# A two-layer transformer on one core: the last expert quad by column halves, the layer border rewritten tile by tile, and the loads of layer 1 in another order

## The reference

```python
c_act = silu(c)
for l in range(2):
    mod = c_act @ mod_w[l] + mod_b[l]                     # 6 rows of 1024
    shift1, scale1, gate1, shift2, scale2, gate2 = split(mod, 6)
    h = rms_norm(x, norm1_g[l]) * (1 + scale1) + shift1
    mix = diff_fox_mixer(h, ...) if l == 0 else stick_breaking_mixer(h, ...)
    x = x + gate1 * mix
    h = rms_norm(x, norm2_g[l]) * (1 + scale2) + shift2
    x = x + gate2 * hier_moe(h, ...)                      # 4 groups of 8 experts

def stick_breaking_mixer(h, w_in, w_out):                 # 16 heads of 64
    q, k, v = split(h @ w_in, 3)
    z = q k^T / 8;  log_keep = where(mask, log_sigmoid(-z), 0)
    later = reverse cumsum(log_keep) - log_keep
    a = where(mask, exp(log_sigmoid(z) + later), 0)
    return (a @ v) @ w_out

hid = silu(h @ w1[e]) * (h @ w3[e])                       # per expert, D=1024 -> 512
y  += (hid * gate) @ w2[e]                                # 512 -> 1024
```

## Time and profile before

| | us |
|---|---|
| median of three runs | 1255.74 (1253.07 to 1257.35) |
| the profiled execution, its own time | 1254.81 |
| its span on the core | 1252.7 |
| PE busy | 909.3 |
| DVE busy | 299.1 |
| ACT busy | 197.6 |
| DMA, mean over the span | 391 GB/s |

### The profile page before, as it was taken

How to read it: one execution, slowest core, us unless ns; L and a number is a source line. 1 busy time by engine, 2 the same in 40 slices (tenths; PEclk the granted TensorE clock), 3 DMA queues, 4 the chain that set the end, 5 groups by cost and what they waited for, 6 DMA issues and landing times.

```text
span 1252.7 us, 13436 instructions
## 1 busy us (share of the span) xinstructions
PE 909.3 (73%) x5515; PEld 419.7 (34%) x5515; DVE 299.1 (24%) x596; ACT 197.6 (16%) x410; POOL 14.9 (1%) x81
## 2 busy tenths in 40 slices
PE   7999999656565556484889999957556565655578
PEld 3445555122221212131348664522121222213133
DVE  1578634001010101010137555501010010101011
ACT  2213414010100100000020454311010101000000
POOL 4000000000000000000000000000000000000000
PEclk9999999788788878777999999988787888877879
DMA  9998897999999999999999936889999999999997
GB/s 357 362 397 280 326 387 279 419 427 427 431 428 427 427 429 429 429 426 428 419 400 408 370 129 268 345 353 428 428 426 428 429 429 429 427 428 426 428 424 303
DMA packets 74605, 489.95 MB, mean 391 GB/s; under 512 B 18092, under 2 KB 18228, under 8 KB 47680
## 3 DMA queue, kind: packets, MB, share of 16 engines
q1 hardware_dynamic: 74256, 488.25, 94.8%
q10 hardware_dynamic: 304, 1.07, 0.3%
HBM read 488.25 MB, written 1.05 MB: 391 GB/s over the span
## 4 chain that ended last, share of the span: by engine, by line
DMA 49%; PE 43%; DVE 3%; SPq 2%; issue 1%; ACT 1%; DVEq 0%; ACTq 0%
DMA tokens<-in_moe_w_dram 46%; PE bank L1128 13%; PE bank L810 8%; PE bank L1161 5%; PE bank L1009 5%; PE bank L863 4%; SPq L510 2%; DMA ring<-in_moe_w_dram 2%; PE bank L738 1%; DMA ring<-in_mod_w_dram 1%; PE bank L931 1%; PE bank L947 1%; PE bank L1095 1%; PE bank L796 1%; PE bank L1172 1%
## 5 line engine op out<-in xcount | busy, mean ns | idle before, releaser
L1128 PE MATMUL bank<-ring,region 128*32 128x512 f32 x1456 | 263.1, 675 | 173.1 <-DMA tokens<-in_moe_w_dram 91.8
L1161 PE MATMUL bank<-ring,region 128*32 128x512 f32 x832 | 143.9, 719 | 131.9 <-DMA ring<-in_moe_w_dram 77.7
L1128 PEld LDWEIGHTS bank<-ring,region 128*32 128x32 f32 x1456 | 69.3, 122 | 351.9 <-issue 288.5
L1128 PE MATMUL bank<-work,region 128*32 128x512 f32 x256 | 134.1, 685 | 0.0
L1128 PE MATMUL bank<-tokens,region 128*32 128x512 f32 x256 | 134.0, 685 | 0.0
L2123 DVE TENSOR_TENSOR region<-region,bank 128x512 f32<-128x512 f32 x16 | 11.0, 688 | 443.6 <-PE bank L1128 443.6
L810 PE MATMUL bank<-ring,tokens 128*128 128x512 f32 x256 | 114.3, 596 | 0.6 <-ACT tokens L1378 0.6
L1161 PEld LDWEIGHTS bank<-ring,region 128*32 128x32 f32 x832 | 37.2, 129 | 224.2 <-issue 189.3
L2133 DVE TENSOR_TENSOR region<-bank,region 128x512 f32<-128x512 f32 x32 | 22.1, 692 | 262.8 <-PE bank L1161 262.8
L1378 ACT ACTIVATE region<-bank,shift,scale 128x128 f32<-128x128 f32 x64 | 24.1, 457 | 358.4 <-PE bank L1115 358.4
L1115 PE MATMUL bank<-region,h 128*128 128x128 f32 x512 | 64.1, 287 | 9.1 <-issue 8.3
(11 more groups left out here) (280 smaller groups left out, 930.0 us busy)
## 6 DMA issues: line engine op xcount, KB each, us to landing
ring<-in_moe_w_dram SPq DMA_DIRECT2D x132, 2048.0 KB, 19.5
work<-in_moe_w_dram SPq DMA_DIRECT2D x22, 2048.0 KB, 24.3
tokens<-in_moe_w_dram SPq DMA_DIRECT2D x22, 2048.0 KB, 28.6
ring<-in_mod_w_dram SPq DMA_DIRECT2D x20, 2048.0 KB, 13.8
ring<-in_moe_w_dram SPq DMA_DIRECT2D x8, 1536.0 KB, 13.5
ring<-in_od_w_in_dram SPq DMA_DIRECT2D x5, 2048.0 KB, 15.0
ring<-in_mod_w_dram SPq DMA_DIRECT2D x8, 1024.0 KB, 14.4
ring<-in_ev_w_in_dram SPq DMA_DIRECT2D x4, 2048.0 KB, 17.7
```

Of the source, the lines that this page charges most:

```text
L1128: last = pe.matmul(bank[which][32 * j:32 * j + 32, :], m.seated[:, k, 32 * j:32 * j + 32], weights(4 * which + j, k * FE), start=(k == 0), ...
L1161: last = pe.matmul(bank[half][32 * j:32 * j + 32, :], m.hidT[:, c, 32 * j:32 * j + 32], w, start=(c == 0), stop=(c == FC - 1), skip_group_ ...
```

## The change

Three things, in the words of the code:

- **Last quad of a layer.** The last three w2 units come as column halves: first half of c = 1, 2, 3, then the second halves, the very last one in two quarters of 256 columns. TensorE multiplies the first columns for all c and gives these results back at once, then does the other half in two quarters of 256 columns (banks 1 and 2). VectorE makes y in three pieces, the last two of 256 columns.
- **Layer border.** VectorE copies the first halves of x after its last piece of y; ScalarE takes the squares by halves, one of them straight from PSUM; VectorE scales both tiles; the modulation is done in pieces of 128x128, tile by tile, and the first projection takes the pieces in the order in which they come.
- **Order of the loads of layer 1.** `DENSE_ORDER[1]` is another, and three steps at which TensorE and VectorE deal with the `SECOND` sums are put three later.

```diff
-               [("in", 0), (GATE1, 0), (GATE1, 1), ("in", 1), (SECOND, 0), ("in", 2), (SECOND, 1), (SECOND, 2),
-                (SECOND, 3), ("in", 3), ("in", 4), ("in", 5)] + GATE_THEN_OUT]
+               [("in", 0), ("in", 1), ("in", 2), (GATE1, 0), (GATE1, 1), (SECOND, 0), (SECOND, 1), ("in", 3),
+                (SECOND, 2), (SECOND, 3), ("in", 4), ("in", 5)] + GATE_THEN_OUT]
-SECOND_PART_AT = (12, 2)
-SECOND_COLS_AT = (13, 4)
+SECOND_PART_AT = (12, 5)
+SECOND_COLS_AT = (13, 7)
-ADD_SUMS_AT = (17, 1)
+ADD_SUMS_AT = (17, 4)
...
+            landed(8)
+            products_of(0, 0, 0, COL)
+            products_of(0, 1, COL, T)
+            products_of(0, 2, COL + T, T).then_inc(used, 1)
+            for c in range(1, FC):
+                if c >= 2:
+                    keep_clock(3, 3)
+                pe.wait_ge(m.half_full[c - 1], 16 * (l + 1))
+                last = products_of(c, 0, 0, COL)
+            last.then_inc(e["y_half"], 1)
+            pe.wait_ge(e["y_copied"], copied)
+            give_back(0, COL, (end_sem, 1))
+            for c in range(1, FC - 1):
+                if c == 2:
+                    keep_clock(3, 3)
+                landed(8 + c)
+                products_of(c, 1, COL, T)
+                products_of(c, 2, COL + T, T).then_inc(used, 1)
+            keep_clock(3, 3)
+            pe.wait_ge(m.last_full, 16 * (l + 1))
+            products_of(FC - 1, 1, COL, T).then_inc(e["y_half"], 1)
+            landed(QUAD_UNITS - 1)
+            products_of(FC - 1, 2, COL + T, T).then_inc(used, 1)
+            pe.wait_ge(e["y_copied"], copied + 1)
+            give_back(COL, T)
+            pe.wait_ge(e["y_copied"], copied + 2)
+            give_back(COL + T, T, (end_sem, TT))
...
-            if halves and c >= 2:
-                keep_clock(3, 5 if c == 2 else 3)
...
-            keep_clock(2, 10)
+            keep_clock(2, 4)
             turn_tokens(2 * l)
-            keep_clock(2, 2)
+            keep_clock(2, 1)
...
+    def norm_sums():
+        for t in range(TT):
+            act.wait_ge(s["dve_took"], t + 1)
+            chain.link(fn(m.h[:, t, 0:COL], m.x[:, t, 0:COL], ACT.Square, accum_out=m.sq_sum[:, 2 + t:3 + t]))
+            chain.link(fn(m.sq_sum[:, 4 + t:5 + t], m.sq_sum[:, 2 + t:3 + t], ACT.Identity, scale=1.0 / D,
+                          bias=m.eps[:, 0:1]))
+        for t in range(TT):
+            if t == 0:
+                act.wait_ge(m.moe[0, "end"], 2)
+                fn(m.h[:, 0, COL:D], bank[6][:, :], ACT.Square, accum_out=m.sq_sum[:, 0:1]).then_inc(s["act_took"], 1)
+                act.wait_ge(s["act_took"], 1)
+            else:
+                act.wait_ge(s["dve_took"], 3)
+                chain.link(fn(m.h[:, 1, COL:D], m.x[:, 1, COL:D], ACT.Square, accum_out=m.sq_sum[:, 1:2]))
...
+    def take_sums(l):
+        for t in range(1 if l + 1 == DEPTH else TT):
+            dve.wait_ge(m.moe[l, "end"], 1)
+            dve.tensor_copy(m.x[:, t, 0:COL], bank[4 + t][:, :]).then_inc(s["dve_took"], 1)
...
+        dve.wait_ge(m.moe[l, "end"], 3)
+        dve.tensor_copy(m.x[:, 1, COL:D], bank[7][:, :]).then_inc(s["dve_took"], 1)
+        dve.wait_ge(s["act_took"], 1)
+        dve.tensor_copy(m.x[:, 0, COL:D], bank[6][:, :]).then_inc(s["x_added"], TT)
...
+        for t in range(TT):
+            dve.wait_ge(s["rstd_done"], 3 + t)
+            ts(m.h[:, t, :], m.x[:, t, :], m.rstd[:, t:t + 1], None, ALU.mult).then_inc(
```

More of the change, by code:

```diff
@@ L1144, in quad_of_experts, with products_of, give_back @@
         pe.wait_ge(e["turned_copied"], 2 * n + 2)
+        def products_of(c, b, lo, n):
+            for j in range(4):
+                last = pe.matmul(bank[b][32 * j:32 * j + 32, 0:n], m.hidT[:, c, 32 * j:32 * j + 32],
+                                 weights(8 + c, j * D + lo, n), start=(c == 0), stop=(c == FC - 1),
+                                 skip_group_check=True, tile_position=(0, 32 * j))
+            return last
+        def give_back(lo, n, end=None):
+            half, col = divmod(lo, COL)
+            for t in range(TT):
+                last = pe.matmul(bank[4 + 2 * half + t][:, col:col + n], m.back[:, t, :], m.y_seat[:, lo:lo + n],
+                                 start=False, stop=end is not None, skip_group_check=True)
+                if end is not None and t >= TT - end[1]:
+                    last.then_inc(end[0], 1)
@@ L1146, in quad_of_experts @@
+        if lead_fill:
+            pe.wait_ge(m.lead_full, lead_fill)
+        for j in range(4):
+            landed(8 + j)
         for c in range(FC):
-            if c == 0 and not halves:
-                if lead_fill:
-                    pe.wait_ge(m.lead_full, lead_fill)
+            for half in range(2):
                 for j in range(4):
-                    landed(8 + j)
-            if halves and c >= 2:
-                keep_clock(3, 5 if c == 2 else 3)
[L1154 to L1161, removed]
+                    last = pe.matmul(bank[half][32 * j:32 * j + 32, :], m.hidT[:, c, 32 * j:32 * j + 32],
+                                     weights(8 + j, c * D + half * COL),
@@ L1169, in quad_of_experts @@
         for half in range(2):
[L1170 to L1175, removed]
+            pe.wait_ge(e["y_copied"], 2 * n + half + 1 + ended)
+            give_back(half * COL, COL)
     def experts(l):
@@ L1642, in program_scalar @@
     for half in range(OUT_UNITS):
-        act.wait_ge(m.moe[DEPTH - 1, "end"], half + 1)
-        act.copy(m.x[:, 1, half * COL:(half + 1) * COL], bank[5 + 2 * half][:, :]).then_inc(s["y1_ready"], 1)
+        act.wait_ge(m.moe[DEPTH - 1, "end"], 2 * half + 1)
+        act.copy(m.x[:, 1, half * COL:(half + 1) * COL], bank[5 + 2 * half][:, :]).then_inc(s["act_took"], 1)
 def backwards(ap):
@@ L2126, in quad_of_experts @@
             e["turned_copied"], 1)
-        for half in range(OUT_UNITS):
-            if half == 0:
-                dve.wait_ge(e["y_half"], n + 1)
+        ended = l if path == "first" else 0
+        pieces = ((0, 0, COL), (1, COL, T), (2, COL + T, T)) if last else ((0, 0, COL), (1, COL, COL))
+        for i, (b, lo, cols) in enumerate(pieces):
+            if i + 1 < len(pieces):
+                dve.wait_ge(e["y_half"], n + 1 + ended + i)
             else:
                 wait_used(dve, m, l, path, n, 12)
-            cols = slice(half * COL, (half + 1) * COL)
-            tt(m.y_seat[:, cols], bank[half][:, :], m.gate2[:, cols], ALU.mult).then_inc(e["y_copied"], 1)
+            tt(m.y_seat[:, lo:lo + cols], bank[b][:, 0:cols], m.gate2[:, lo:lo + cols], ALU.mult).then_inc(
+                e["y_copied"], 1)
+        if last:
+            return
         dve.wait_ge(e["gate_made"], n + 1)
```

129 lines of the change are left out of this document (77 added, 52 removed).

## The result

The changed kernel takes 1275.72 us (median of 4 runs, 1273.24 to 1276.35) against 1255.7 before (1253.07 to 1257.35): a ratio of 1.0163, with a 95% interval of 1.0147 to 1.0180. It is slower by 20 us. The forecast was 1271.5, with a range from 1264 to 1277. Its profiled execution took 1276.27, with a span of 1274.5 against 1252.7.

The account below looks back on a forecast made before the run. Bound: PE in layer 1's dense stage, bytes in its expert stage. Terms -1.6 + 13.5 + 1.0 - 0.55 + 1.7 + 2.3 = +16.35 on 1254.81 gave 1271.2, stated as 1271.5; range 1264 to 1277.

Parts of the forecast that it names:

- the order of loads: Layer 1 dense stage: late third SECOND unit delays VectorE's sums and heads; TensorE waits 14.4 us, second scores +13.5.
- The clock's term: Work behind TensorE's wait in layer 1's dense stage runs partly at 1.2 GHz: +1.7 us, ends 0.5 and 4.
- 1.0 for add_sums, -0.55: Layer 1 dense stage, behind the second scores: add_sums paid later, +1.0 us; a wait at 716.57 goes, -0.55.
- the last quad of layer 1: Column halves lengthen TensorE's own work from 14.86 to 17.55 us, +2.7, less 0.4 for stores: +2.3.
- the start of the projections: Layer border: reworked copies, squares and pieces let projections start near 653.8, 1.6 us before 655.43; ends 0 and 3.
- (a): Layer 1 dense stage: late sums hold nobody, so not slower; 5 in 100 for 1256, 3 for faster.
- (b): Wait before second scores costs more: lower clock +4 for 1.7, wait 15 us; 1275 to 1277; 13 in 100.
- (c): Part given back: last quads free and border gives 3, 1267; or SECOND loads 3 us sooner, 1265; 14 in 100.
- (d): Last-quad halves fail their purpose in either layer, as PE, not loads, ends the quad; already in the forecast.

Follow-up runs that it names:

- the first two runs: Kernel before with only the new load order and its three step constants: 1272.19 us, 1.0134; changed kernel with old order and constants: 1258.67 us, 1.0030.
- the last pair: Changed kernel, old load order, no keep_clock in last quads, with 8 instead of 4 keep_clock matmuls before border transposes: 1249.43 us; same without that edit: 1249.75 us.
- the best version: Changed kernel with the old load order and without the 12 keep_clock matmuls in each layer's last quad: 1249.47 us, ratio 0.9947; run again 1249.75, 0.9964.

## Why the prediction was right, and where it was off

**The step that decided, the order of loads, held.** The prediction had 65.75 us from the first projection to the second scores, the profile has 65.55. Landing after 8.0 us: 7.2 here. Sums at 5.27 a unit: 10.53 for two. VectorE's wait for the load: some 17 forecast, 19.96 measured. TensorE's wait: 14.4 forecast, 13.96 measured. That VectorE's sums are the link, and not the late units as such, is shown by the run with the sums between the heads; that the table alone does it, by the run with the table alone.

**The clock's term held**: 1.7 us, at the scores and the projection behind them, and the run with 31 keep_clock matmuls takes it away. A second fall was not in the sum: from the second scores to the experts the profile has +3.6 where the prediction had +2.15 (1.0 for add_sums, -0.55, 1.7). The difference lies in the row at 821.11, 1.84 for 0.94, and that at 822.95, 4.23 for 3.43. This fall is not shown to come from the change (last section).

**The first term that was mis-sized: the last quad of layer 1**, +2.7 less 0.4 for the stores in the prediction, +3.8 and 0 in the profile. I had taken a keep_clock matmul at 0.47, from five in a row; in threes it is 0.50, so the increase is 2.1 and not 1.9. I had taken the groups at 0.91, from four in a row; between other work they take 1.00 (so too in layer 0 before, where the waits for loads were 1.13 and 1.01, 2.1 us, and not the 2.4 that I got by subtraction). Giving back in parts takes 0.33 more than in one go, which I had left out. And the stores had not waited for one another: each landed 2.2 us after its issue in both kernels. The mechanism was right, with TensorE as the end of the quad, and is now shown: without the 12 matmuls the loads are the bound and the quad is 6 us shorter.

**The second: the start of the projections**, 1.6 us earlier in the prediction and 0.8 later in the profile. Of the 2.4 us, 0.84 lie ahead of the whole change (the first w2 product of layer 0 at 630.40 for 629.56; the other runs lie between 629.0 and 633.0), 1.1 is the same mis-sized quad in layer 0, and 0.5 a slower border: the transposes took 2.77 for 2.05, with the clock down. The border itself gains about what was forecast (8.6 us less 6.7, so 1.9), 2.0 us in the profile where it stands alone.

In all the profile has +21.8 for the sum's +16.35. The 5.45 between them are 2.4 for the start of the projections, 1.45 up to the experts, 1.1 and 0.4 for the last quad and the stores, 0.3 for the expert stage, and 0.2 less for the wait.

**The rivals.** (a) falls with the first two runs. (b), a longer wait or a longer fall of the clock at it, is not what happened, though the median, 1275.72, lies in its band (1275 to 1277) and 0.7 above the forecast's own (1268 to 1275). The wait was 14.0 and not 15, and the clock cost 1.7 there; another 1.7 in the routing and 0.7 at the border were falls that the prediction does not name. That the time came out inside the whole range is owed to the decisive step; that it did so in (b)'s part of it is owed to terms that (b) doesn't have. (c) falls: nothing is given back, the expert stage takes 418.3 us for 418.0. (d), that the halves do nothing for either layer as written, held: with their keep_clock they cost 0.61%, by the sum that follows.

The sum by the runs: the order +1.34%, the border -0.31%, the halves with their keep_clock, as the difference between 1.0030 and 0.9969, +0.61%.

## What to carry to other kernels

A unit of a ring doesn't only have its own place in an order of loads: it inherits the slot of the unit one turn before it, and with the slot the engine that frees it. Moving two early units ("in" 1 and 2) forward gave nothing, since nobody had waited for them, and it moved a late one, the third of SECOND, from a slot freed by VectorE (issue by 667.1) to one freed 30 us later by TensorE (698.19). Before an order is changed, write down for each unit who frees its slot, when, and what stands behind its consumer in that engine's program.

Filler matmuls are free only while something else is the bound. Whoever shortens the path behind the last load has to take the filler out with it, or else the filler becomes the bound. The price is a clock that may fall at the waits that open up, as it did in two of these profiles (without keep_clock in the kernel before, and in the first of the last pair); both runs of the last pair are faster than the kernel before all the same.

## What the hardware showed that I had not expected

In the run with 26 filler matmuls the clock fell at the 2.97 us of waiting behind them, and it was at the lower level (0.65 and 0.50 in the windows 724 to 728) exactly when the work came back. Filling 11.4 us of a 14 us wait was worth nothing that could be measured; filling 13.5 us took 1.7 us out of the rows behind it. That is one profile each, and a wait alone doesn't decide: at the border TensorE waits 1.83 us ahead of the transposes in five kernels alike, and the clock falls there in three profiles (transposes of 2.77, 2.53 and 2.78 us) and not in two (2.05 and 2.07).

In the changed kernel, with the order alone and with 26 matmuls the clock fell once more, some 100 us after the first time, in the routing between 820 and 827, where TensorE waits for nothing over 0.7 us. It costs 1.7 us there. In the kernel before, with the order undone, with the sums between the heads and with 31 matmuls it did not, which looks as if the second fall followed from the first. It doesn't have to: the clock also fell at this place in the kernel before without keep_clock, with the border alone, and in the second profile of the best version, and in none of these had it fallen since the border. With the border alone this row of the timeline takes 4.43 us, where the kernel before has 3.60:

```profile
804.76 4.43 PE L1110 MATMUL bank<-tokens,ident 128*128 128x512 f32 x8
```

The first profile of the same best version has no fall there. So it comes and goes between executions of one kernel, and what decides it stays open.
